# Turning round the up products of the dense feed-forwards

## The chip, the cores and the metric

One NeuronCore of a Trainium2 chip runs the whole program. The metric is the device time of an execution in microseconds. Three executions of the kernel before gave 2583.58, 2585.54 and 2586.75 us; the median is 2585.54.

## What is computed

Four transformer layers over 256 tokens of width 1024. Each has a mixer of four branches and then a feed-forward. Layers 1 to 3 have a dense one, layer 4 has eight experts, of which each token takes two. The change is about the three dense ones:

```
def swiglu(h, w_in, w_out):
    gate, up = jnp.split(h @ w_in, 2, axis=-1)
    return (jax.nn.silu(gate) * up) @ w_out
x = x + swiglu(rms_norm(x, g), w_in, w_out)      # hidden width 2816
```

`rms_norm` divides each token by the root mean square of its 1024 values and multiplies by a gain of each channel.

## The kernel before

**Precision.** Every large product is made of three in the fp32r form: with a = a_hi + a_lo and b = b_hi + b_lo, it adds a_hi b_hi, a_lo b_hi and a_hi b_lo. `hi` is a rounded copy, which ScalarE makes (`conv` in its program, recorded at line 1286, the helper's line), and `lo` the remainder, which VectorE makes (line 1685).

**The weight stream.** All weights are laid out as chunks of 128 x 2048 values (1 MB) in the order of use. SyncE loads them into a ring of six (`raw`); ScalarE makes `w_hi` in a ring of three; VectorE writes the remainder over the raw chunk. `conv(c + 2)` stands beside chunk c in both programs. TensorE waits for `lo_ready` of a chunk and counts `w_used` when done; that count releases ring places.

**Norm.** TensorE turns x into channel-major form, and ScalarE and VectorE write `xhi` and `xlo` (128 channels x 8 groups x 256 tokens) with the gain but without the division by the root mean square. ScalarE computes 1/rms of each token into `nstat` columns 4 and 5, token on the partition, after it has delivered `xhi`. So the factor is applied later, where a product leaves its PSUM bank.

**A dense stage.** The hidden width is cut into J = 11 blocks of 256. A block has two up chunks (each half of the 1024 input channels, for 256 gate and 256 up columns) and one down chunk (256 hidden rows by 1024 outputs). `feed_forward` in the programs of TensorE (line 1110), ScalarE (1568) and VectorE (2137) is driven by one order, `walk` (line 569): first up chunk of block j+1, turn of block j, second up chunk of block j+1, down chunk of block j. The middle blocks stand in a hardware loop of two blocks.

- Up (`gemm_half`, line 707): x is stationary, a 128 x 128 load for each group of channels and 128 tokens, and 512 weight columns move: 24 products in a chunk, recorded at lines 716 to 718. The result has tokens on partitions, one bank for each 128 tokens, gate in columns 0 to 255 and up in the others.
- Gating: ScalarE writes `silu` = Silu(gate x 1/rms) from PSUM, VectorE `gprod` = up x 1/rms x silu (line 2145), 128 tokens at a time; 1/rms is a value of each partition.
- Turn: TensorE transposes `gprod` in four 128 x 128 pieces (line 705) into the banks of the block, ScalarE rounds them to `ghi`, VectorE writes `glo` (line 2152).
- Down (`gemm_rows`, line 721): `ghi` and `glo` are stationary, 512 weight columns move, 24 products (lines 731 to 733), adding up in banks 4 to 7 over all blocks. In the last chunk each half of the columns is counted apart, and VectorE adds them to x.

Blocks take turns between banks 0, 1 and 2, 3; `claim`, `use`, `ev` and `fl` plan which use of a bank waits for which release. The routed experts have their own functions and lines (1185 to 1206, 2204, 2208). The narrow projection of the mixers (lines 806 to 808) multiplies 28 stationary weight columns by 256 moving tokens.

Of the kernel before, what the change touches and what calls it, by code (L numbers as in the profile page):

```python
# [15 lines left out]
P = 128  # L16
# [204 lines left out]
def program(nc, a, out, stop=99):  # L221

    ctx = ExitStack()
    with ctx:
# [33 lines left out]

        pick = sb("pick", [P, NT, P], at=u_at + 8192)
# [152 lines left out]
        silu_done, ghi_done = sem("silu_done"), sem("gated_hi")  # L412
        route_m, route_e = sem("route_max"), sem("route_exp")
# [27 lines left out]
        USE, FULL, CH, FFB, HALF = {}, {}, {}, {}, {}  # L441
# [35 lines left out]
        for k in phases:  # L477
# [32 lines left out]
            else:  # L510
                J = FFJ[k[0]]
                FFB[k] = ffb
                if k[0] == "moe":
# [12 lines left out]
                    JU, JF = [m - n for m, n in zip(uses, u0)], [m - n for m, n in zip(fulls, f0)]  # L526
                    claim((k, "turned"), X[2])
                    claim((k, "scatter"), X[2], X[3], 2, 3)
                    c += 2
                else:  # L530
                    for j in range(J):
                        for t in range(NT):
                            claim((k, "U", j), 2 * (j % 2) + t, streamed=True)
                            claim((k, "T", j), 2 * (j % 2) + t)
                    claim((k, "D"), *X, streamed=True)
                    HALF[k, "D"] = len(HALF) + 1
                    c += 3 * J
                    ffb += 2 * J
                    last_x = [(b, USE[(k, "D"), b] + 1) for b in X]
# [160 lines left out]
        def _(pe):  # L700
# [409 lines left out]
            def feed_forward(k, J):  # L1110
                c0 = CH[k]

                def up(j, it, c, half):
# [5 lines left out]
                    if half == 0:  # L1119
                        for b in banks:  # L1120
                            pe.wait_ge(free[b], use((k, "U", j), b) + 2 * it)
                    gemm_half(banks, c0 + c, 4 * half, half == 0, half == 1, it)

                def turn(j, it):
                    for t in range(NT):
                        b = gbank(j, t)

                        pe.wait_ge(free[b], use((k, "T", j), b) + 2 * it)
                        tr(bank[b][:, 0:P], gprod[:, t, 0:P])
                        tr(bank[b][:, P:2 * P], gprod[:, t, P:2 * P]).then_inc(full[b], 1)  # L1130

                def down(j, it, c):
# [6 lines left out]
                    gemm_rows(X, c0 + c, lambda kk, t: (ghi[:, kk, t, :], glo[:, kk, t, :]), j == 0, j == J - 1, it,  # L1139
                              by_half=j == J - 1)  # L1140

                walk(pe, J, lambda j, it, c: up(j, it, c, 0), turn, lambda j, it, c: up(j, it, c, 1), down)
# [133 lines left out]
        def _(act):  # L1276
# [291 lines left out]
            def feed_forward(k, J):  # L1568
                c0 = CH[k]

                def up_done(j, it, c):
                    conv(c0 + c + 2, it)
                    for t in range(NT):
                        act.wait_ge(w_used, c0 + c + 1 + 6 * it)
                        go(silu[:, t, :], bank[gbank(j, t)][:, 0:FB], ACT.Silu, scale=nstat[:, 4 + t:5 + t]).then_inc(silu_done, 1)

                def turn(j, it):
                    for t in range(NT):
                        b = gbank(j, t)
                        act.wait_ge(full[b], fl((k, "T", j), b) + it)  # L1580
                        go(ghi[:, :, t, :], bank[b][:, 0:FB].rearrange("p (a b) -> p a b", a=2), ACT.Copy).then_inc(ghi_done, 1)
# [88 lines left out]
        def _(dve):  # L1670
# [466 lines left out]
            def feed_forward(k, J):  # L2137
                c0, f0 = CH[k], FFB[k]

                def up_done(j, it, c):  # L2140
                    conv(c0 + c + 2, it)
                    for t in range(NT):
                        b = gbank(j, t)
                        dve.wait_ge(silu_done, f0 + 2 * j + t + 1 + 4 * it)
                        V.scalar_tensor_tensor(out=gprod[:, t, :], in0=bank[b][:, FB:2 * FB], scalar=nstat[:, 4 + t:5 + t],
                                               in1=silu[:, t, :], op0=ALU.mult, op1=ALU.mult).then_inc(free[b], 1)

                def turn(j, it):
                    for t in range(NT):
                        b = gbank(j, t)  # L2150
                        dve.wait_ge(ghi_done, f0 + 2 * j + t + 1 + 4 * it)
                        V.tensor_tensor(glo[:, :, t, :], bank[b][:, 0:FB].rearrange("p (a b) -> p a b", a=2),  # L2152
                                        ghi[:, :, t, :].bitcast(F32), ALU.subtract).then_inc(free[b], 1)
# [422 lines left out]
```

## Time and profile before

| | |
|---|---|
| median of three executions | 2585.54 us |
| profiled execution | 2585.76 us, span 2583.9 us |
| TensorE, its weight loads | 2509.5 us (97%), 2068.5 us (80%) |
| VectorE | 1818.7 us (70%) |
| ScalarE | 1521.9 us (59%) |
| GpSimd | 183.6 us (7%) |
| read from and written to HBM | 626.57 MB, 7.48 MB |

The profile is of one execution. PE is TensorE and PEld its weight loads, which overlap its products. A product's recorded length of 0.39 us is longer than the distance to the next start, as products are pipelined; distances between starts are what counts. Spans of the other engines are true lengths. "Idle before" is the time that an engine stood before an instruction, with the one that released it.

### The profile page before, as it was taken

How to read it: one execution, taken by the hardware profiler on the slowest of the kernel's cores; microseconds unless marked ns; L12 is line 12 of the kernel's file. 1: busy time of each engine (PE TensorE's matmuls, PEld its weight loads, DVE VectorE, ACT ScalarE, POOL GpSimd, SP SyncE). 2: the span in 40 equal slices, each digit the busy share in tenths (PEclk: the TensorE clock that was granted, in tenths of full speed). 3: DMA queues.
4: the chain of work that ended last, by engine and by line, in shares of the span. 5: the costliest groups of instructions: out<-in, count | busy, mean ns of one | idle time of the engine just before them, and what ended most of it. 6: DMA issues, size and time to landing. Idle time of an engine off the chain costs nothing.

```text
span 2583.9 us, 32235 instructions
## 1 busy us (share of the span) xinstructions
PE 2509.5 (97%) x11900; PEld 2068.5 (80%) x11900; DVE 1818.7 (70%) x1795; ACT 1521.9 (59%) x1581; POOL 183.6 (7%) x141
## 2 busy tenths in 40 slices
PE   6999999999999999999999998999999999999997
PEld 5888788788878878878888876888888888888876
DVE  5577754557775555665555467888888888888887
ACT  5455544454544354545445555777777777777766
POOL 0100200010020000020000012000000000000060
PEclk8999999999999999999999999999999999999999
DMA  6444455444445564545554455999999999999995
GB/s 220 147 147 163 166 192 183 161 160 151 163 163 187 187 205 151 180 164 179 193 181 161 163 179 206 364 370 383 380 377 374 376 385 376 383 368 386 373 361 224
DMA packets 90564, 635.24 MB, mean 246 GB/s; under 512 B 10477, under 2 KB 10853, under 8 KB 15472
## 3 DMA queue, kind: packets, MB, share of 16 engines
q1 hardware_dynamic: 85104, 617.41, 65.0%
q0 software_dynamic: 4896, 16.09, 1.8%
q8 instruction: 56, 0.92, 0.1%
q10 hardware_dynamic: 480, 0.59, 0.1%
q14 instruction: 28, 0.23, 0.0%
HBM read 626.57 MB, written 7.48 MB: 245 GB/s over the span
## 4 chain that ended last, share of the span: by engine, by line
PE 88%; DVE 4%; ACT 3%; issue 3%; DMA 1%; DVEq 0%; SPq 0%; ACTq 0%
PE bank L716 13%; PE bank L718 12%; PE bank L717 12%; PE bank L1206 7%; PE bank L1204 7%; PE bank L1205 7%; PE bank L1185 4%; PE bank L1187 4%; PE bank L1186 4%; PE bank L731 3%; PE bank L733 3%; PE bank L732 3%; PE bank L705 3%; DVE w_lo L1685 2%; ACT w_hi L1286 1%
## 5 line engine op out<-in xcount | busy, mean ns | idle before, releaser
L1685 DVE TENSOR_TENSOR w_lo<-raw,w_hi 128x2048 fp32r<-128x2048 f32 x586 | 1359.2, 2322 | 492.5 <-ACT w_hi L1286 480.0
L1286 ACT ACTIVATE w_hi<-raw 128x2048 fp32r<-128x2048 f32 x586 | 1121.6, 1915 | 269.2 <-PE bank L733 102.1
L716 PE MATMUL bank<-w_hi,xhi 128*128 128x512 f32 x1456 | 580.4, 399 | 13.2 <-DVE w_lo L1685 7.5
L718 PE MATMUL bank<-w_lo,xhi 128*128 128x512 f32 x1456 | 569.7, 391 | 0.0
L717 PE MATMUL bank<-w_hi,xlo 128*128 128x512 f32 x1456 | 569.4, 391 | 0.0
L1204 PE MATMUL bank<-w_hi,xhi 128*128 128x512 f32 x896 | 359.0, 401 | 2.4 <-DVE w_lo L1685 2.4
L1206 PE MATMUL bank<-w_lo,xhi 128*128 128x512 f32 x896 | 350.2, 391 | 0.0
L1205 PE MATMUL bank<-w_hi,xlo 128*128 128x512 f32 x896 | 349.5, 390 | 0.0
L716 PEld LDWEIGHTS bank<-w_hi,xhi 128*128 128x128 f32 x1456 | 274.9, 189 | 71.8 <-issue 12.5
L718 PEld LDWEIGHTS bank<-w_lo,xhi 128*128 128x128 f32 x1456 | 274.6, 189 | 58.9
L717 PEld LDWEIGHTS bank<-w_hi,xlo 128*128 128x128 f32 x1456 | 275.2, 189 | 54.0
L1206 PEld LDWEIGHTS bank<-w_lo,xhi 128*128 128x128 f32 x896 | 168.2, 188 | 35.7
L1204 PEld LDWEIGHTS bank<-w_hi,xhi 128*128 128x128 f32 x896 | 168.3, 188 | 35.3 <-DVE w_lo L1685 3.9
L1286 ACT ACTIVATE ghi<-bank 128x256 fp32r<-128x256 f32 x178 | 64.8, 383 | 219.2 <-PE bank L705 219.2
L1205 PEld LDWEIGHTS bank<-w_hi,xlo 128*128 128x128 f32 x896 | 168.7, 188 | 31.6
L1185 PE MATMUL bank<-w_hi,ghi 128*128 128x512 f32 x448 | 176.9, 395 | 10.7 <-DVE glo L2208 10.7
L1186 PE MATMUL bank<-w_hi,glo 128*128 128x512 f32 x448 | 175.1, 391 | 0.0
L1187 PE MATMUL bank<-w_lo,ghi 128*128 128x512 f32 x448 | 175.1, 391 | 0.0
L2447 POOL TENSOR_TENSOR u<-u,gates 128x512 f32<-128x512 f32 x32 | 61.1, 1938 | 705.6 <-DVE gates L2091 705.6
L1185 PEld LDWEIGHTS bank<-w_hi,ghi 128*128 128x128 f32 x448 | 84.5, 189 | 32.5 <-DVE w_lo L1685 12.3
L731 PE MATMUL bank<-w_hi,ghi 128*128 128x512 f32 x264 | 103.0, 390 | 3.3 <-DVE glo L2152 3.3
L733 PE MATMUL bank<-w_lo,ghi 128*128 128x512 f32 x264 | 102.8, 389 | 0.0
(364 smaller groups left out, 2462.8 us busy)
## 6 DMA issues: line engine op xcount, KB each, us to landing
raw<-in_wexpert SPq DMA_DIRECT2D x337, 1024.0 KB, 5.1
raw<-in_wdense SPq DMA_DIRECT2D x249, 1024.0 KB, 4.8
expert_rows<-y POOLq DMA_DIRECT2D x7, 512.0 KB, 4.5
expert_rows<-back POOLq DMA_DIRECT2D x3, 512.0 KB, 3.8
x<-in_x SPq DMA_DIRECT2D x2, 512.0 KB, 4.9
biasT<-bias_rows POOLq DMA_DIRECT2D x1, 1024.0 KB, 6.7
normal_rows<-hrow POOLq DMA_DIRECT2D x1, 1024.0 KB, 6.3
out<-hrow SPq DMA_DIRECT2D x2, 512.0 KB, 2.7
```

What stands on the lines that cost most here:

```text
L716: mm(bank[banks[t]][:, :], xhi[:, k0 + k, tok], wh, start=start and k == 0, stop=False)
L717: mm(bank[banks[t]][:, :], xlo[:, k0 + k, tok], wh, start=False, stop=False)
L718: last = mm(bank[banks[t]][:, :], xhi[:, k0 + k, tok], wl, start=False, stop=stop and k == 3)
L731: mm(b, xh, hi[:, h, o:o + 512], start=first and k == 0, stop=False)
L1185: mm(dst, ghi[:, m, 0, :], hi[:, h, w], start=first, stop=False)
L1186: mm(dst, glo[:, m, 0, :], hi[:, h, w], start=False, stop=False)
L1187: last = mm(dst, ghi[:, m, 0, :], lo[:, s, w], start=False, stop=final)
L1204: mm(bank[b][:, :], xhi[:, kt, 0:P], hi[:, h, w], start=kt == 0, stop=False)
L1205: mm(bank[b][:, :], xlo[:, kt, 0:P], hi[:, h, w], start=False, stop=False)
L1206: last = mm(bank[b][:, :], xhi[:, kt, 0:P], lo[:, s, w], start=False, stop=kt == KT - 1)
L1286: return nc.scalar.activation(dst, src, f, **kw)
L1685: V.tensor_tensor(lo[:, c % RAW, :], raw[:, c % RAW, :], hi[:, c % HI, :].bitcast(F32), ALU.subtract).then_inc(lo_ready, 1)
```

## The change

The up products swap operands. The 128 x 128 weight tile is stationary and 256 tokens of x move, so that a chunk has 48 products of 256 columns in place of 24 of 512. The result has hidden channels on partitions: the gate in one bank (two groups of 128 channels by 256 tokens), up in the other. The gated product is thus in the form that the down product needs, and the four transposes are gone. 1/rms of a token lies along the free axis now. A row of it on all partitions (`rrow`) is made once a stage: VectorE scales an identity by it (`diag`), TensorE multiplies that by ones after the first up chunk, VectorE copies the bank. Then VectorE multiplies gate and up by the row, ScalarE takes Silu of the scaled gate, VectorE multiplies, ScalarE rounds (`fhi`) and VectorE writes the remainder (`flo`), each over 128 x 512 values at once. The fourth layer's experts are as before. Cut to its core:

```diff
+        fhi = sb("fhi", [P, 2, S], F32R, at=u_at)
+        flo = sb("flo", [P, 2, S], F32R, at=u_at + 2048)
         ...
+                    claim((k, "rstd"), X[0])
                     for j in range(J):
                         for t in range(NT):
                             claim((k, "U", j), 2 * (j % 2) + t, streamed=True)
-                            claim((k, "T", j), 2 * (j % 2) + t)
@@ TensorE, up
-                    gemm_half(banks, c0 + c, 4 * half, half == 0, half == 1, it)
-                def turn(j, it):
-                    for t in range(NT):
-                        b = gbank(j, t)
-                        pe.wait_ge(free[b], use((k, "T", j), b) + 2 * it)
-                        tr(bank[b][:, 0:P], gprod[:, t, 0:P])
-                        tr(bank[b][:, P:2 * P], gprod[:, t, P:2 * P]).then_inc(full[b], 1)
+                    pe.wait_ge(lo_ready, i + 1 + 6 * it)
+                    for kk in range(4):
+                        row = 4 * half + kk
+                        for m in range(4):
+                            w = slice(kk * 512 + m * P, kk * 512 + m * P + P)
+                            o = bank[banks[m // 2]][:, m % 2 * S:m % 2 * S + S]
+                            mm(o, hi[:, h, w], xhi[:, row, :], start=row == 0 and m % 2 == 0, ...)
+                            mm(o, hi[:, h, w], xlo[:, row, :], start=False, ...)
+                            last = mm(o, lo[:, s, w], xhi[:, row, :], start=False, ...)
+                    last.then_inc(w_used, 1)
+                    if j == 0 and half == 0:
+                        b = X[0]
+                        pe.wait_ge(free[b], use((k, "rstd"), b))
+                        pe.wait_ge(diag_ready, DIAG[k])
+                        for t in range(NT):
+                            last = mm(bank[b][:, t * P:t * P + P], C("ones"), diag[:, t, :], start=True, stop=True)
+                        last.then_inc(full[b], 1)
@@ TensorE, down
-                    for t in range(NT):
-                        b = gbank(j, t)
-                        pe.wait_ge(free[b], ev((k, "T", j), b) + 2 * it)
+                    pe.wait_ge(glo_done, FFB[k] + j + 1 + 2 * it)
@@ ScalarE
-                        go(silu[:, t, :], bank[gbank(j, t)][:, 0:FB], ACT.Silu, scale=nstat[:, 4 + t:5 + t]).then_inc(silu_done, 1)
+                    b = gbank(j, 0)
+                    act.wait_ge(free[b], ev((k, "U", j), b) + it)
+                    go(fsilu[:, :, :], gscaled[:, :, :], ACT.Silu).then_inc(silu_done, 1)
@@ ScalarE, turn
-                        go(ghi[:, :, t, :], bank[b][:, 0:FB].rearrange("p (a b) -> p a b", a=2), ACT.Copy).then_inc(ghi_done, 1)
+                    if j > 0:
+                        act.wait_ge(w_used, c0 + 3 * j + 2 + 6 * it)
+                    act.wait_ge(prod_done, FFB[k] + j + 1 + 2 * it)
+                    go(fhi[:, :, :], fprod[:, :, :], ACT.Copy).then_inc(ghi_done, 1)
@@ VectorE
+                dve.wait_ge(norm_rstd, NORM[k])
+                for t in range(NT):
+                    last = V.tensor_scalar(diag[:, t, :], ident_t[:, :], nstat[:, 4 + t:5 + t], None, ALU.mult)
+                last.then_inc(diag_ready, 1)
+                def per_token(dst, b):
+                    return V.tensor_tensor(dst, bank[b][:, :].rearrange("p (m t) -> p m t", m=2),
+                                           rrow[:, :].unsqueeze(1).to_broadcast([P, 2, S]), ALU.mult)
@@ VectorE, behind the second up chunk
+                    if j == 0:
+                        wait_full((k, "rstd"), X[0])
+                        V.tensor_copy(rrow[:, :], bank[X[0]][:, 0:S]).then_inc(free[X[0]], 1)
+                        dve.wait_ge(free[X[0]], ev((k, "rstd"), X[0]))
+                    dve.wait_ge(w_used, c0 + c + 1 + 6 * it)
+                    per_token(gscaled[:, :, :], gbank(j, 0)).then_inc(free[gbank(j, 0)], 1)
+                    per_token(uscaled[:, :, :], gbank(j, 1)).then_inc(free[gbank(j, 1)], 1)
+                    dve.wait_ge(free[gbank(j, 1)], ev((k, "U", j), gbank(j, 1)) + it)
+                    dve.wait_ge(silu_done, f0 + j + 1 + 2 * it)
+                    V.tensor_tensor(fprod[:, :, :], uscaled[:, :, :], fsilu[:, :, :], ALU.mult).then_inc(prod_done, 1)
@@ VectorE, turn
+                    dve.wait_ge(ghi_done, f0 + j + 1 + 2 * it)
+                    V.tensor_tensor(flo[:, :, :], fprod[:, :, :], fhi[:, :, :].bitcast(F32), ALU.subtract).then_inc(glo_done, 1)
```

## Rows read from the trace of the kernel before

**Rows 1.** The page: engines' busy time (part 1) and the chain by engine (part 4).

```profile
PE 2509.5 (97%) x11900; PEld 2068.5 (80%) x11900; DVE 1818.7 (70%) x1795; ACT 1521.9 (59%) x1581; POOL 183.6 (7%) x141
...
PE 88%; DVE 4%; ACT 3%; issue 3%; DMA 1%; DVEq 0%; SPq 0%; ACTq 0%
```

**Rows 2.** Windows of the first dense stage: busy us and instructions, clock, DMA share, GB/s.

```profile
304.00:490.00 186.00, 184.45 (x834) 152.64 (x835) 96.55 (x84) 84.59 (x90) 0.00 (x0) 1.00 0.53 183
```

**Rows 3.** TensorE's timeline in that stage (start us, us, engine, line, operation).

```profile
326.81 0.39 PE L731 MATMUL bank<-w_hi,ghi 128*128 128x512 f32 x1
...
332.25 0.39 PE L716 MATMUL bank<-w_hi,xhi 128*128 128x512 f32 x1
...
337.69 0.60 PE L705 MATMUL bank<-ident_t,gprod 128*128 128x128 f32 x4
338.05 0.48 PE L716 MATMUL bank<-w_hi,xhi 128*128 128x512 f32 x1
338.36 0.39 PE L717 MATMUL bank<-w_hi,xlo 128*128 128x512 f32 x1
...
354.49 0.60 PE L705 MATMUL bank<-ident_t,gprod 128*128 128x128 f32 x4
```

**Rows 4.** The timeline at the last turn of that stage.

```profile
483.16 0.40 PE L733 MATMUL bank<-w_lo,ghi 128*128 128x512 f32 x1
...
485.08 0.47 PE L731 MATMUL bank<-w_hi,ghi 128*128 128x512 f32 x1 [1.09 <-DVE glo L2152]
```

**Rows 5.** Groups by line and form: count, busy us, mean ns, idle before.

```profile
L2135 DVE TENSOR_TENSOR x<-bank,x 128x512 f32<-128x512 f32 x16 | 10.0, 684 | 0.0
...
L1286 ACT ACTIVATE kq<-E 128x512 fp32r<-128x512 f32 x2 | 1.2, 616 | 0.0
...
L2025 DVE TENSOR_SCALAR P2m<-P2m,small 128x256 f32<-128x256 f32 x8 | 2.8, 348 | 0.0
```

**Rows 6.** TensorE's timeline, narrow projection: first, 24th, and the product behind.

```profile
23.92 0.28 PE L806 MATMUL bank<-xhi,wsm_hi 128*28 128x256 f32 x1
...
26.59 0.28 PE L808 MATMUL bank<-xhi,wsm_lo 128*28 128x256 f32 x1
26.71 0.40 PE L716 MATMUL bank<-w_hi,xhi 128*128 128x512 f32 x1
```

**Rows 7.** TensorE's timeline, 256 and 128 columns in turn: first of 16, next after.

```profile
198.75 0.28 PE L925 MATMUL bank<-tri,zhi 128*128 128x256 f32 x1
...
200.51 0.45 PE L716 MATMUL bank<-w_hi,xhi 128*128 128x512 f32 x1
```

**Rows 8.** The weight loads' timeline in the same stretch.

```profile
198.75 0.19 PEld L926 LDWEIGHTS bank<-tri,zhi 128*128 128x128 f32 x1
198.87 0.19 PEld L925 LDWEIGHTS bank<-tri,zlo 128*128 128x128 f32 x1
198.97 0.19 PEld L926 LDWEIGHTS bank<-tri,zlo 128*128 128x128 f32 x1
```

**Rows 9.** The timeline of all engines at the start of the first dense stage.

```profile
309.84 0.44 ACT L1286 ACTIVATE nstat<-nstat 128x2 f32<-128x2 f32 x2
310.01 0.39 PE L716 MATMUL bank<-w_hi,xhi 128*128 128x512 f32 x1
...
312.26 2.29 DVE L1685 TENSOR_TENSOR w_lo<-raw,w_hi 128x2048 fp32r<-128x2048 f32 x1 [6.34 <-ACT w_hi L1286]
```

**Rows 10.** TensorE's timeline, plain f32 products with a full load.

```profile
69.12 1.89 PE L835 MATMUL bank<-z,cst 128*128 128x256 f32 x8
70.66 0.58 PE L716 MATMUL bank<-w_hi,xhi 128*128 128x512 f32 x1
```

**Rows 11.** Timelines of ScalarE and VectorE in the block of rows 3.

```profile
327.74 1.92 ACT L1286 ACTIVATE w_hi<-raw 128x2048 fp32r<-128x2048 f32 x1
332.45 1.92 ACT L1286 ACTIVATE w_hi<-raw 128x2048 fp32r<-128x2048 f32 x1 [2.80 <-PE bank L733]
...
329.68 2.29 DVE L1685 TENSOR_TENSOR w_lo<-raw,w_hi 128x2048 fp32r<-128x2048 f32 x1 [1.29 <-ACT w_hi L1286]
```

More of the change, by code:

```diff
@@ L512, in program @@
                 FFB[k] = ffb
+                DIAG[k] = len(DIAG) + 1
+                NORM[k] = len([p for p in phases[:phases.index(k)] if p[0] == "norm"])
                 if k[0] == "moe":
@@ L537, in program @@
                     c += 3 * J
-                    ffb += 2 * J
+                    ffb += J
                     last_x = [(b, USE[(k, "D"), b] + 1) for b in X]
@@ L1120, in up @@
                         for b in banks:
-                            pe.wait_ge(free[b], use((k, "U", j), b) + 2 * it)
-                    gemm_half(banks, c0 + c, 4 * half, half == 0, half == 1, it)
-                def turn(j, it):
-                    for t in range(NT):
-                        b = gbank(j, t)
-                        pe.wait_ge(free[b], use((k, "T", j), b) + 2 * it)
-                        tr(bank[b][:, 0:P], gprod[:, t, 0:P])
-                        tr(bank[b][:, P:2 * P], gprod[:, t, P:2 * P]).then_inc(full[b], 1)
+                            pe.wait_ge(free[b], use((k, "U", j), b) + it)
+                    i = c0 + c
+                    s, h = i % RAW, i % HI
+                    pe.wait_ge(lo_ready, i + 1 + 6 * it)
[4 more added lines that the diff above has]
+                            o = bank[banks[m // 2]][:, m % 2 * S:m % 2 * S + S]
+                            mm(o, hi[:, h, w], xhi[:, row, :], start=row == 0 and m % 2 == 0, stop=False, skip_group_check=True)
+                            mm(o, hi[:, h, w], xlo[:, row, :], start=False, stop=False, skip_group_check=True)
+                            last = mm(o, lo[:, s, w], xhi[:, row, :], start=False, stop=row == KT - 1, skip_group_check=True)
+                    last.then_inc(w_used, 1)
[6 more added lines that the diff above has]
+                        last.then_inc(full[b], 1)
                 def down(j, it, c):
@@ L1135, in down @@
                             pe.wait_ge(free[b], use((k, "D"), b))
[L1136 to L1139 removed]
+                    pe.wait_ge(glo_done, FFB[k] + j + 1 + 2 * it)
+                    gemm_rows(X, c0 + c, lambda kk, t: (fhi[:, kk, t * P:t * P + P], flo[:, kk, t * P:t * P + P]), j == 0, j == J - 1, it,
                               by_half=j == J - 1)
[L1142 removed]
+                walk(pe, J, lambda j, it, c: up(j, it, c, 0), lambda j, it: None, lambda j, it, c: up(j, it, c, 1), down)
             def gather(k):
@@ L2140, in up_done @@
                 def up_done(j, it, c):
                     conv(c0 + c + 2, it)
[L2142 to L2146, printed above, removed]
-                def turn(j, it):
[L2149 to L2153, printed above, removed]
+                    if j == 0:
+                        wait_full((k, "rstd"), X[0])
+                        V.tensor_copy(rrow[:, :], bank[X[0]][:, 0:S]).then_inc(free[X[0]], 1)
+                        dve.wait_ge(free[X[0]], ev((k, "rstd"), X[0]))
```

14 lines of the change are left out of this document (8 added, 6 removed).

## The prediction

> **What bounds the kernel now.** I read the page first, then stages by windows, then TensorE's timeline inside one stage. The page shows TensorE busy for 97% of the span and 88% of the chain of waits on it, vector and scalar engines far behind [rows 1]. The three dense feed-forward stages are each about 186 us long; in the first TensorE is busy 184.45 us of 186 at a granted clock of 1.00 (2.4 GHz), VectorE 96.6 and ScalarE 84.6, DMA at 0.53 [rows 2]. So only what TensorE issues, or what makes it wait, counts there; a longer vector instruction costs nothing while it stays inside its slack.
>
> One steady block of a stage shows it [rows 3]. The 24 products of the down chunk start at 326.81 and the next chunk's first at 332.25: 5.44 us, 0.2267 us for each 512-column product, with its weight load hidden. From the first turn to the next, 337.69 to 354.49, a block takes 16.80 us. It holds 72 such products, 72 x 0.2267 = 16.32. The rest, 0.48 us, is the turn: four transposes from 337.69, and the product behind them, whose successor starts 0.31 us later instead of 0.227.
>
> **Part by part.** A stage has 11 blocks, 22 up chunks and 11 down chunks.
>
> *Turns removed.* Ten of the eleven turns stand in a stream that never waits, so each gives back 0.48 us less rounding, 0.475: 3 x 10 x 0.475 = 14.2 us. The eleventh, before the last down chunk, is different. Now the last product of block 9 starts at 483.16 and the last down chunk at 485.08 [rows 4], and the transposes lie inside a wait for copy and remainder. After the change the same place holds no transposes, but the rounding copy may start only when that product has ended (its buffer is single): 483.56 + ScalarE's copy of 512 columns 0.62 + VectorE's subtraction 0.68 [rows 5] + three handovers of about 0.05 = 485.0. Gain nothing. Nor is anything behind it: VectorE and ScalarE queue there only the next stage's first conversions.
>
> *Up products turned round.* Each up chunk had 24 products of 512 columns with a 128-column load of x; it gets 48 of 256 columns with a 128-column load of weights. Columns streamed stay the same, loads double. If t is the spacing of the new ones, the stages pay 66 x (48t - 24 x 226.7 ns), which is 3168 x (t - 113.35 ns). This one number decides the case, and no row shows exactly that product, so I bound it:
> - The narrow projection has the same form (weights stationary, hi twice, lo once, x moving, 256 columns) but loads 28 columns: 24 of them from 23.92 to 26.71, 116.25 ns each [rows 6].
> - Products of 256 and 128 columns in turn, both with 128-column loads: 16 from 198.75 to 200.51, 110 ns each [rows 7]. In the loads' own timeline a load beside a 256-column product is followed by the next after 0.12 us, one beside a 128-column product after 0.10 [rows 8]. So a full load needs less than the 113 ns, but with the wide product on top the pair takes up to 0.12.
> - Lower end: half of 226.7, 113.35 ns, since per column nothing in the stages is cheaper: cost 0. A gain below that is left out, as the columns are the same. Upper end: 120 ns, cost 21.1 us.
> I take 115.5 ns, nearest to the first row and a little under it, because that run is short and lies between wider products, and feed-forward stages are the steadiest stretches of the trace: 3168 x 2.15 = 6.8 us. Both ends go into the range.
>
> The rows show 0.2267 us for 512 columns [rows 3] and 116.25 ns for 256 [rows 6]. The Trainium skill (TensorE: Matmul & The Clock Gate, "Back-to-back issue gap") gives a warm gap of N/2.4 + 2.5 ns for an isolated product, 215.8 and 109.2 ns, so doubling the count would cost 2.5 ns for each old product, 4 us in all (an estimate from the page). The same section warns that in a stream of load and product pairs both set the spacing, and puts 128-column products at about 81 ns where the gap alone is 56; that speaks against this change, and is taken up below.
>
> *Changing width.* Where TensorE goes from short products back to 512-column ones the first steps are longer [rows 3]. This happens once in a block: 0 to 1.5 us in all, I take 1.0.
>
> *Scaling moved behind the product.* Token scales now lie along the free axis, so a row of them is made once a stage: VectorE waits for the reciprocal root, makes two diagonal tiles, TensorE multiplies them by ones after its first up chunk, VectorE copies the bank. The root's instruction ends at 310.06 (two in 0.44 us from 309.84) [rows 9]; two 128-column scalings at some 0.22 each (256 columns take 0.35 [rows 5]) end at 310.5, so TensorE can go on at 310.6. Its first chunk ended at 310.01. It stalls 0.6, runs two f32 products of 128 columns at 0.11 (eight of 256 take 1.54 us to the next start [rows 10]) and restarts its stream, 0.1 to 0.2: about 1.0 us a stage, 3.0 in all; 0.7 if the diagonal were ready, 4.5 if each handover took twice as long. Queued behind VectorE's new wait is its conversion of the third chunk, which started at 312.26 as ScalarE had not delivered before [rows 9], so it is not moved.
>
> *Vector and scalar work.* After an up chunk VectorE does two scalings of 512 columns from PSUM (0.68 each), ScalarE Silu of 512 from SBUF (0.62) beside the second, VectorE the product (0.68) [rows 5]: ready some 2.1 us after the chunk instead of 1.4. Before it, in queue, is the conversion at 327.74 on ScalarE and 329.68 on VectorE [rows 11]; they move by some 0.6 us. That conversion is for the chunk that TensorE begins at 338.05 [rows 3] and was done at 331.97: 6 us of slack. Rounding and remainder no longer wait for the transposes at 337.69 [rows 3]; they follow the conversion that ScalarE starts at 332.45 [rows 11], so they come earlier than now. TensorE's work covers all of this; without that cover it would be 0.6 us a block, 20 us. Banks come free earlier. DMA order and volume stay as they are.
>
> **Sum.** -14.2 + 6.8 + 1.0 + 3.0 = -3.4 us. The profiled execution took 2585.76 us with a span of 2583.9; that is 0.2 above the median of the three runs, 2585.54. The forecast is 2585.76 - 3.4 = 2582.4 us. About 0.2%, 5.2 us, is what a measurement can tell from no change. By the sum, the spacing gives a gain beyond that under 114.9 ns, and a loss beyond it over 118.2 ns.
>
> **Rivals.**
> *The split is free.* Long runs of short products settle at 113.35 to 114.5 ns. For: the stages' wide products hold 226.7 block after block [rows 3]; the load alone needs less. Against: 116.25 over 24 products in the narrow projection, at a much smaller load [rows 6]. Time 2575.6 at 113.35, up to 2579.2.
> *The load becomes the bound (slower).* Every product now has a full load beside its whole length. The load rows show 0.12 us for just this [rows 8], and if it holds for all 3168 the split costs 16 to 21 us where the turns give back 14.2. It decides from 118.2 ns on. At 118.5 the time is 2591.9, at 120 it is 2596.6. For: it is the only row with both sizes. Against: those loads follow short ones, and their first wide product has none of it.
> *The load is hidden only in part.* At 125 ns the split costs 36.9 us and the time is 2612.5. The run of 16 products at 110 ns speaks against it [rows 7]. The page's rule above, carried over as 25 ns on top of 109 (an estimate), would be 134 ns and some 65 us; this case's rows, at 116.25 with small loads, don't agree with it.
> *The gated product is late.* If remainders came after the down chunk's turn, each block would wait. Per block 1 us late gives 33 us, 2615. Against: 6 us of slack at each step.
> *That it doesn't do what it says* would be equal weights in a row loaded once, with only 32 loads in a chunk. The narrow projection's hi weights stand twice in a row too and each product there has its own load; it would only help, and is the free split.
>
> **Chances.** Forecast (114.9 to 118.2 ns) 0.39, own range 2580 to 2591; free split 0.36; load as bound 0.20; partly hidden 0.03; late product 0.02. So faster 0.36, same 0.39, slower 0.25. The range takes the free split and its uncertain small terms at one end and the load bound at 120 ns at the other: 2573 to 2597.
>
> **What would show it.** Right: transposes of the gated product gone from the dense stages, a block of 16.5 to 16.6 us with up products 115 to 116 ns apart, TensorE waiting once a stage for about 0.6 us on the diagonal, the last down chunk still starting some 1.9 us after the last product before it. Free split: blocks of 16.35. Load as bound: 16.9 and more, loads touching each other on TensorE's load row. The forecast is wrong if TensorE waits inside the loop for VectorE or ScalarE, if chunks after the first wait for conversions, or if the change of width costs more than 0.05 us a block.

## The result, and the profile after it

The changed kernel takes 2598.71 us (median of five runs, 2595.79 to 2599.49) against 2585.54 for the kernel before (five runs, 2583.58 to 2591.5). The ratio is 1.0048, 95% interval 1.0036 to 1.0059: slower by half a per cent. The forecast was 2582.4.

The page of the changed kernel, parts 1 and 4, answers to [rows 1]. TensorE has 1464 products more and 9 us more of busy time, VectorE 34 us more, and the chain lies on TensorE as before:

```profile
PE 2518.7 (97%) x13364; PEld 2139.8 (82%) x13364; DVE 1852.3 (71%) x1804; ACT 1514.5 (58%) x1515; POOL 188.7 (7%) x141
...
PE 87%; ACT 4%; DVE 4%; issue 3%; DMA 1%; DVEq 0%; SPq 0%; ACTq 0%
```

Its groups by line and form (busy us, mean ns, idle before). The up products, 3168 in three lines of 1056 each, wait 3.0 us in the whole program; the transposes of gated products fell from 356 to 224, the experts' own:

```profile
L1142 PE MATMUL bank<-xhi,w_hi 128*128 128x256 f32 x1056 | 299.1, 283 | 3.0 <-DVE xlo L1715 3.0
...
L743 PE MATMUL bank<-w_hi,fhi 128*128 128x512 f32 x264 | 103.4, 392 | 4.3 <-DVE flo L2184 4.3
```

The block of [rows 3] in TensorE's timeline. Line 743 begins a down chunk, line 1142 an up chunk:

```profile
328.43 0.40 PE L743 MATMUL bank<-w_hi,fhi 128*128 128x512 f32 x1
...
333.90 0.28 PE L1142 MATMUL bank<-xhi,w_hi 128*128 128x256 f32 x1
334.01 0.28 PE L1143 MATMUL bank<-xlo,w_hi 128*128 128x256 f32 x1
334.13 0.28 PE L1144 MATMUL bank<-xhi,w_lo 128*128 128x256 f32 x1
334.25 0.28 PE L1142 MATMUL bank<-xhi,w_hi 128*128 128x256 f32 x1
...
345.41 0.40 PE L743 MATMUL bank<-w_hi,fhi 128*128 128x512 f32 x1
```

From down chunk to down chunk 16.98 us, 16.80 before. The two up chunks fill 333.90 to 345.41: 11.51 us for 96 products, 119.9 ns each, without a wait or a transpose among them. Before, the same columns took 48 x 226.7 ns = 10.88 us and the turn 0.48. The weight loads go at the same pace, one for each product. Their records of 0.19 us are longer than the distance of 0.12 between them, so the loads' row has no gap any more:

```profile
350.99 0.19 PEld L1144 LDWEIGHTS bank<-xhi,w_lo 128*128 128x128 f32 x1
351.11 0.19 PEld L1142 LDWEIGHTS bank<-xhi,w_hi 128*128 128x128 f32 x1
```

Windows in up chunks (span, busy us of the loads, clock, DMA share, GB/s), the changed kernel first, then the kernel before:

```profile
335.00:345.00 10.00, 10.00 (x85) 1.00 0.63 211
```

```profile
333.00:337.00 4.00, 3.31 (x18) 1.00 0.81 266
```

The start of the stage, where the row of scales is made (compare [rows 9]), and the last turn ([rows 4]):

```profile
310.01 0.48 DVE L2162 TENSOR_SCALAR diag<-ident_t,nstat 128x128 f32<-128x128 f32 x2 [4.17 <-ACT nstat L1306]
310.09 0.28 PE L1144 MATMUL bank<-xhi,w_lo 128*128 128x256 f32 x1
...
310.64 0.68 PE L1151 MATMUL bank<-diag,cst 128*128 128x128 f32 x4 [0.27 <-DVE diag L2162]
311.08 0.36 PE L1142 MATMUL bank<-xhi,w_hi 128*128 128x256 f32 x1
...
486.49 0.39 PE L745 MATMUL bank<-w_lo,fhi 128*128 128x512 f32 x1
...
486.91 0.63 ACT L1306 ACTIVATE fhi<-fprod 128x512 fp32r<-128x512 f32 x1 [2.30 <-PE bank L745]
...
487.57 0.69 DVE L2184 TENSOR_TENSOR flo<-fprod,fhi 128x512 fp32r<-128x512 f32 x1 [0.64 <-ACT fhi L1306]
...
488.32 0.50 PE L743 MATMUL bank<-w_hi,fhi 128*128 128x512 f32 x1 [1.44 <-DVE flo L2184]
```

The second chunk starts 0.87 us late (311.08 against 310.09 + 0.12). The last turn takes 1.83 us, 1.92 before.

**Where the 13 us are.** I measure a dense stage from its norm's first transpose to that of the next norm. Before it is 189.47, 189.48 and 189.50 us; after, 192.84, 192.82 and 192.83. That is 10.0 us in all. The mixers between them are equal within 0.1 us, what lies ahead of the first within 0.4. The other 3.1 us of the two profiled spans lie in the expert stage (1005.73 and 1008.85), whose code is the same. TensorE's clock is part of it: windows there (columns: span, busy us of PE, PEld, DVE, ACT, POOL, clock, DMA share, GB/s) show 3.4 us at half clock (1.2 GHz). TensorE had stood idle for 3.0 us, up to 1623.83, and then worked for 1.2 us at the full clock. First the changed kernel:

```profile
1620.00:1625.00 5.00, 2.00 (x9) 1.39 (x8) 4.83 (x9) 2.47 (x3) 2.53 (x2) 1.00 0.96 377
1625.00:1628.40 3.40, 3.40 (x9) 2.62 (x9) 3.30 (x3) 0.04 (x1) 0.00 (x0) 0.50 0.49 159
```

The kernel before, at the same place, has the wait (2.8 us) and not the slow clock:

```profile
1610.00:1615.00 5.00, 2.21 (x10) 1.54 (x9) 4.90 (x6) 2.29 (x3) 1.20 (x2) 1.00 0.96 379
1615.00:1618.40 3.40, 3.40 (x17) 2.80 (x16) 2.89 (x3) 1.92 (x1) 0.00 (x0) 1.00 0.48 175
```

Nine products in 3.4 us instead of seventeen: 1.7 us for one such stretch. The changed kernel's five times themselves lie at 2595.8 and 2595.9 or at 2598.7 to 2599.5, and the profile is of one of the longer ones. So 10 us, those of the dense stages, are the edit's price for certain; whether it has a part in the 3.1 us of the expert stage is taken up in numbers 6 and 7.

### The profile page after: what moved, and what is told of

Read it like the earlier page. It is cut to its first block, busy times and chain, and to the rows that moved or that the text cites. A ratio compares the mean times of both kernels' runs of the same rounds, so it can differ in the third digit from the quotient of the medians.

```text
span 2597.1 us, 35091 instructions
## 1 busy us (share of the span) xinstructions
PE 2518.7 (97%) x13364; PEld 2139.8 (82%) x13364; DVE 1852.3 (71%) x1804; ACT 1514.5 (58%) x1515; POOL 188.7 (7%) x141
## 4 chain that ended last, share of the span: by engine, by line
PE 87%; ACT 4%; DVE 4%; issue 3%; DMA 1%; DVEq 0%; SPq 0%; ACTq 0%
PE bank L728 8%; PE bank L730 8%; PE bank L729 8%; PE bank L1226 7%; PE bank L1224 7%; PE bank L1225 7%; PE bank L1144 5%; PE bank L1143 5%; PE bank L1142 5%; PE bank L1205 4%; PE bank L1207 4%; PE bank L1206 4%; PE bank L743 3%; PE bank L744 3%; PE bank L745 3%
## 5 line engine op out<-in xcount | busy, mean ns | idle before, releaser
L728 PE MATMUL bank<-w_hi,xhi 128*128 128x512 f32 x928 | 371.5, 400 | 10.7 <-DVE w_lo L1705 8.0
L730 PE MATMUL bank<-w_lo,xhi 128*128 128x512 f32 x928 | 363.7, 392 | 0.0
L729 PE MATMUL bank<-w_hi,xlo 128*128 128x512 f32 x928 | 363.5, 392 | 0.0
L1224 PE MATMUL bank<-w_hi,xhi 128*128 128x512 f32 x896 | 359.2, 401 | 3.8 <-DVE w_lo L1705 3.8
L1226 PE MATMUL bank<-w_lo,xhi 128*128 128x512 f32 x896 | 350.2, 391 | 0.0
L1225 PE MATMUL bank<-w_hi,xlo 128*128 128x512 f32 x896 | 349.4, 390 | 0.0
L1142 PE MATMUL bank<-xhi,w_hi 128*128 128x256 f32 x1056 | 299.1, 283 | 3.0 <-DVE xlo L1715 3.0
L1144 PE MATMUL bank<-xhi,w_lo 128*128 128x256 f32 x1056 | 298.8, 283 | 0.0
L1143 PE MATMUL bank<-xlo,w_hi 128*128 128x256 f32 x1056 | 298.8, 283 | 0.0
L1142 PEld LDWEIGHTS bank<-xhi,w_hi 128*128 128x128 f32 x1056 | 202.6, 192 | 4.7 <-DVE xlo L1715 3.6
L1143 PEld LDWEIGHTS bank<-xlo,w_hi 128*128 128x128 f32 x1056 | 202.6, 192 | 1.1
L1144 PEld LDWEIGHTS bank<-xhi,w_lo 128*128 128x128 f32 x1056 | 202.6, 192 | 0.0
L1205 PE MATMUL bank<-w_hi,ghi 128*128 128x512 f32 x448 | 177.4, 396 | 10.4 <-DVE glo L2239 10.4
```

The costliest lines, as they stand in the source:

```text
L728: mm(bank[banks[t]][:, :], xhi[:, k0 + k, tok], wh, start=start and k == 0, stop=False)
L729: mm(bank[banks[t]][:, :], xlo[:, k0 + k, tok], wh, start=False, stop=False)
L730: last = mm(bank[banks[t]][:, :], xhi[:, k0 + k, tok], wl, start=False, stop=stop and k == 3)
L1142: mm(o, hi[:, h, w], xhi[:, row, :], start=row == 0 and m % 2 == 0, stop=False, skip_group_check=True)
L1143: mm(o, hi[:, h, w], xlo[:, row, :], start=False, stop=False, skip_group_check=True)
L1144: last = mm(o, lo[:, s, w], xhi[:, row, :], start=False, stop=row == KT - 1, skip_group_check=True)
```

## Experiments

Theory A: a 256-column product behind a full weight load is spaced at 120 ns, whatever the surroundings, so cutting a 512-column product in two costs 13.3 ns. Theory B: the 120 ns come from what is special here (which operand is stationary, banks, reads beside it). Theory C: the loss is not in TensorE's stream but in the longer chain of vector and scalar work or in the row of scales.

**1. Products alone.** A kernel of nothing but fp32r products, 48 of each width and load in a row:

```diff
+            for cols in (128, 96, 64, 32):
+                for width in (384, 320, 256, 192, 128):
+                    for _ in range(12): one(128, 512)
+                    for _ in range(48): one(cols, width)
```

> A kernel of its own, with TensorE alone at work: 48 fp32r products in a row for each pair of widths (stationary columns 128, 96, 64, 32; moving columns 512, 384, 320, 256, 192, 128), each product with its own load; it leaves the model's computation out. Theory A, a fixed price for each product that is fed by a full load: spacing is columns / 2.4 ns + 13.3, so 226.7 at 512, 173.3 at 384, 146.7 at 320, 120.0 at 256, and the load's own pace of 108 at 192 and 128; with narrower stationary tiles the price should shrink if it belongs to the load (about 110 at 256 x 32), and stay if it belongs to the product. Rival B, the load is the bound and is slowed by the product beside it: 120 at 256 but also about 120 at 192, and 384 and 320 at the proportional 170 and 142. Rival C, 120 is special to the feed-forward stages (other engines reading the same tiles): 113.3 at 256 here.

TensorE's windows of 5 us each (busy us, products, clock). The count is two or three above 5 us divided by the spacing, as products that began before are in it. This trace has no record of the clock, so that its column reads 1.00 throughout; that these windows are at the full clock shows in the opening products of 512 columns, which are 427 ns apart at first and 227 from 15.2 us on. In order: load of 128 columns beside 384, 320, 256 and 192 moving ones, then loads of 96, 64 and 32 beside 256:

```profile
28.00:33.00 5.00, 5.00 (x31) 1.00 0.01 3
37.00:42.00 5.00, 5.00 (x36) 1.00 0.00 0
47.00:52.00 5.00, 5.00 (x44) 1.00 0.02 3
55.10:60.10 5.00, 5.00 (x48) 1.00 0.00 0
92.30:97.30 5.00, 5.00 (x46) 1.00 0.00 0
135.50:140.50 5.00, 5.00 (x46) 1.00 0.00 0
177.20:182.20 5.00, 5.00 (x45) 1.00 0.01 3
```

Mean distance of starts over the last 36 of each run of 48, ns (512 with the full load: the opening products behind their slow start):

| load \ moving | 512 | 384 | 320 | 256 | 192 | 128 |
|---|---|---|---|---|---|---|
| 128 columns | 226.7 | 173.3 | 146.7 | 120.0 | 111.7 | 111.7 |
| 96 | 230.0 | 175.0 | 146.7 | 116.0 | 90.0 | 85.0 |
| 64 | 230.0 | 173.3 | 146.7 | 113.3 | 88.5 | 60.0 |
| 32 | 231.7 | 173.3 | 143.3 | 117.8 | 88.3 | 60.0 |

Theory A holds for the full load with no other engine at work: the spacing is columns / 2.4 GHz plus 13.3 ns at 512, 384, 320 and 256 columns, and 111.7 ns at 192 and 128, the same for both widths and so the load's own pace (108 was expected). That is against rival B, which had 120 at 192, and rival C, which had 113.3 at 256. What did not come out is that the price belongs to the load. At 320 columns and more a narrower load takes off 3.4 ns at most, and at 512 it adds 3 to 5; at 256 it takes off 6.7 ns at 64 columns, but only 2.2 at 32, where about 110 was expected. So the size of the load decides at 256 columns, not in general. And 256 columns beside the full load take 120.0 ns although 111.7 (the load's pace) and 113.3 (256 columns beside a load of 64) are both shorter.

**2. Only the split.** The kernel before, x stationary as ever, each 512-column up product cut in two:

```diff
-                    gemm_half(banks, c0 + c, 4 * half, half == 0, half == 1, it)
+                            for n in range(2):
+                                w = slice(kk * 512 + n * S, kk * 512 + n * S + S)
+                                o = bank[banks[t]][:, n * S:n * S + S]
+                                mm(o, xhi[:, row, tok], hi[:, h, w], ...)
+                                ...
```

> The kernel before, with each dense up product of 512 columns cut into two of 256; x stays stationary, the turns stay, nothing else changes. Theory A (the doubled number of loads and products is the whole loss, whichever operand is stationary): 120.0 ns between products, 66 chunks x 0.32 = +21.1 us, about 2606.7. Rival (the loss comes from having the weights stationary, or from the new vector chain): products at 113.4 ns and a time within 2 us of the kernel before, 2585 to 2588.

2608.39 us, ratio 1.0085, interval 1.0071 to 1.0099. Each dense stage is 196.26 us, 6.8 longer: 20.3 us. Its timeline has a block of 17.41 us, and 96 up products from 332.63 to 344.57 with a turn between:

```profile
327.16 0.40 PE L731 MATMUL bank<-w_hi,ghi 128*128 128x512 f32 x1
...
332.63 0.28 PE L1132 MATMUL bank<-w_hi,xhi 128*128 128x256 f32 x1
332.74 0.28 PE L1133 MATMUL bank<-w_hi,xlo 128*128 128x256 f32 x1
332.86 0.28 PE L1134 MATMUL bank<-w_lo,xhi 128*128 128x256 f32 x1
...
344.57 0.40 PE L731 MATMUL bank<-w_hi,ghi 128*128 128x512 f32 x1
```

The split alone, with turns kept and no new vector work, loses more than the whole change. Theory B's first part (the side that is stationary) is out; its others (banks, reads beside it) fell with number 1, which has 120.0 ns with nothing beside it.

**3. Only the turns taken out.** The kernel before without the transposes; the down chunk takes the gated product with tokens on partitions, so its values aren't those of the reference.

```diff
-                        tr(bank[b][:, 0:P], gprod[:, t, 0:P])
-                        tr(bank[b][:, P:2 * P], gprod[:, t, P:2 * P]).then_inc(full[b], 1)
+                    pass
```

> The kernel before without the dense transposes: the gated product is rounded straight from SBUF in token-major form, so the down product gets the untransposed matrix (this is the part left out). Up products are the 512-column ones. By my sum the 30 turns are worth 14.2 us and the last one of a stage nothing: 2571.3. Rival (turns lie partly beside other work and are worth less, so that they and not only the split explain the loss): 2574 to 2580.

2572.59 us, ratio 0.9947, interval 0.9934 to 0.9961. A stage is 184.5 us, 4.95 shorter: 14.9 us in all, of which the last turns give 0.7 (1.69 us instead of 1.92 each). The gain that the change was credited with is there; a steady block takes 16.32 us, 0.473 less than with its turn.

**4. The row of scales one chunk later.** The changed kernel, where TensorE takes the diagonal after its second up chunk:

```diff
-                    if j == 0 and half == 0:
+                    if j == 0 and half == 1:
```

> The changed kernel with the row of token scales made after the second up chunk of a stage in place of after the first, so that TensorE no longer waits for the diagonal. Theory: the stall of 0.55 us behind the first chunk goes in three stages, -1.3 us against the changed kernel, 2597.4, if the vector chain of the first block, which then begins 0.2 us later, stays covered. Rival: the row comes too late for the first block and the stall turns up before the first down chunk; no gain, 2598.7.

2596.03 us, ratio to the kernel before 1.0042 (1.0029 to 1.0056). The stages are 192.33, 0.5 shorter: the wait for the diagonal goes, its own products stay. That is 1.5 us in all, 1.3 expected. So the row costs little: 0.87 us a stage as it stood, 2.6 of the 10 us, of which this run gives back the 1.5.

**5. Wide where two share a load.** `x_hi` and `x_lo` beside each other, so that w_hi multiplies both in one product of 512 columns and only w_lo x_hi has 256. ScalarE and VectorE add the halves.

```diff
-                            mm(o, hi[:, h, w], xhi[:, row, :], ...)
-                            mm(o, hi[:, h, w], xlo[:, row, :], ...)
+                            mm(o[:, :], hi[:, h, w], xboth[:, :, row, :], ...)
-                            last = mm(o, lo[:, s, w], xhi[:, row, :], ...)
+                            last = mm(o[:, 0:S], lo[:, s, w], xhi[:, row, :], ...)
```

> The changed kernel, with w_hi multiplied by x_hi and x_lo in one product of 512 moving columns (two halves of a bank) and w_lo by x_hi in one of 256: 16 products of each kind in an up chunk in place of 48 of 256. A block fills four banks, the first block of a stage those of the down product; ScalarE copies the second halves out, VectorE adds them to the first; the row of token scales is made inside the second up chunk. Theory (a price of 13.3 ns for each product with a full load): 16 x (226.7 + 120.0) = 5.55 us a chunk against 5.76 in the changed kernel and 5.44 before; with the turns gone (-14.2), +7.0 for the chunks and +1.5 for the rows of scales the time is some 5.7 us under the kernel before, 2580.5. Rival: banks come free too late (copies and additions take 2.5 us behind each second up chunk, covered by 5.4 us of the down chunk), TensorE waits in each block, and it is no faster than the kernel before.

2596.69 us, ratio 1.0046 (1.0032 to 1.006): a miss by 16 us. Two things failed that the trace shows. In TensorE's timeline a pair takes 0.353 us, not 226.7 + 120.0 = 346.7 ns:

```profile
339.75 0.40 PE L1147 MATMUL bank<-xboth,w_hi 128*128 128x512 f32 x1
339.99 0.28 PE L1148 MATMUL bank<-xboth,w_lo 128*128 128x256 f32 x1
340.11 0.40 PE L1147 MATMUL bank<-xboth,w_hi 128*128 128x512 f32 x1
```

And the last turn took 3.01 us, as VectorE's remainder was queued behind a weight conversion that came too late to be done before it:

```profile
484.73 2.29 DVE L1721 TENSOR_TENSOR w_lo<-raw,w_hi 128x2048 fp32r<-128x2048 f32 x1 [1.04 <-ACT w_hi L1320]
486.94 0.68 DVE L2205 TENSOR_TENSOR flo<-fprod,fhi 128x512 fp32r<-128x512 f32 x1
```

The pairs cost 66 x 16 x 6.1 ns = 6.4 us and the last turns 3 x 1.2 = 3.5. Down chunks of 5.50 us, 5.44 before, account for about 2 more. The rest of the miss is not traced.

**6 and 7. Both kernels again**, unchanged, to see what the expert stage does by chance.

> The changed kernel once more, on the same chip as the run with wide hi products. The three dense stages should take 192.8 us each again, as they hang on 120.0 ns alone. The expert stage, whose code no edit touches, took 1005.7 us in the profile before and 1008.9 in the one after. If that is chance (the place of idle stretches in the clock's steps), it should come out anywhere from 1005 to 1009; if the change causes it, at 1008.5 to 1009 again.

> The kernel before once more, for a second profile: dense stages 189.5 us each. If the length of the expert stage is chance it lies anywhere from 1005 to 1009; if the change lengthens it, at 1005.7 again.

The changed kernel: 2595.97 us, ratio 1.004 (1.0027 to 1.0054), dense stages 192.84 again, expert stage 1009.38 in its profile. The kernel before: one run, 2583.86, stages 189.47, expert stage 1006.08. Both came out where the expectations put them if the change lengthens the expert stage, so these two runs do not show chance.

Other traces speak for it. Number 2, which is the kernel before but for the split, has 1008.29 there, and number 9 1008.77; number 4, the changed kernel but for the place of one step, has 1006.31, and the remaining ones 1005.2 to 1007.0. The four long stages (the two of the changed kernel, numbers 2 and 9) each have a stretch of 3.4 us at half clock some 36.5 us behind their start, and the eight others have none there. The ten times of the changed kernel in both sets fall in two groups, six at 2595.4 to 2596.3 and four at 2598.7 to 2599.5, and both its profiles are of the upper one. So the same kernel takes either time; what decides it is not shown, nor whether the change makes the longer one more likely.

**8. Products alone, second set.** Other widths, two widths in turn, and in groups of 16:

```diff
+            for width in (288, 240, 224): ...      # load of 128
+            for cols in (112, 80): ...             # beside 256 columns
+            one(128, 512); one(128, 256)           # in turn, then 16 and 16
```

> The kernel of products alone once more, with full loads: 48 products each of 288, 240 and 224 moving columns; 256 columns with stationary tiles of 112 and 80; 512 and 256 in turn; 16 of 512 and then 16 of 256, four times; 512 x 128 and 256 x 64 in turn. Theory A: 133.3 at 288, 113.3 at 240, the floor of 112 at 224; at 256 between 120 and 113.4 as the stationary tile shrinks. For the product pair of 512 and 256 columns, 352 ns in the kernel with wide hi products: if the turn-about of widths costs it, the pair in turn takes 352 here too and 16 and 16 in groups take 226.7 and 120.0 each; if other engines cost it, the pair takes 346.7 here.

Full loads: 131.7 ns at 288 columns (11.7 above columns / 2.4; 133.3 expected), 111.7 at 240 and 224. Beside 256 columns: 117.8 with a load of 112, 113.3 with 80. In turn, 512 and 256 take 353.3 a pair (236.3 and 117.0); in groups they settle at 226.7 and 120.0. So the 6 ns of experiment 5 come from changing width at each product, and grouping takes most of them away: with the first steps of each group in it, a group of 16 and 16 takes 347 to 348 ns for two products. The last part, 512 columns with the full load and 256 with a load of 64 in turn, takes 346.7 a pair (229 and 118). Each alone would give 226.7 + 113.3 = 340.0, so changing width costs 6.7 there as well.

**9. Half a load.** The changed kernel with stationary tiles of 64 columns; half of the hidden channels is left out, the number and width of products stay.

```diff
-                            w = slice(kk * 512 + m * P, kk * 512 + m * P + P)
-                            o = bank[banks[m // 2]][:, m % 2 * S:m % 2 * S + S]
+                            w = slice(kk * 512 + m * P, kk * 512 + m * P + 64)
+                            o = bank[banks[m // 2]][0:64, m % 2 * S:m % 2 * S + S]
```

> The changed kernel with stationary weight tiles of 64 columns in place of 128 in the dense up products; it leaves out half of the hidden channels. The number of products and the 256 moving columns stay. By the spacing kernel the products should be 113.4 ns apart and not 120.0, so a dense stage takes 1056 x 6.6 ns = 7.0 us less, 185.9 us. Rival (the loss comes with 48 products in place of 24 whatever they load): 120.0 ns and 192.8 us.

One run, 2579.64 us; stages 186.26, that is 6.6 less than the changed kernel. In the timeline three steps take 0.35 us; a steady block takes 16.35 us with 113.4 ns for each of its 96 up products:

```profile
333.65 0.28 PE L1142 MATMUL bank<-xhi,w_hi 128*64 128x256 f32 x1
333.77 0.28 PE L1143 MATMUL bank<-xlo,w_hi 128*64 128x256 f32 x1
333.88 0.28 PE L1144 MATMUL bank<-xhi,w_lo 128*64 128x256 f32 x1
334.00 0.28 PE L1142 MATMUL bank<-xhi,w_hi 128*64 128x256 f32 x1
```

With nothing changed but the columns of the stationary tile, the stage gets back nearly all of the 7.0 us that the split cost (22 x 0.32). That is the free split of the prediction, down to its block of 16.35 us. So the cause is in the stationary tile and not in the number of products: the full tile beside 256 columns costs 6.6 ns over 113.4. A tile of 64 columns is a smaller load and also half as many rows of output, and no run separates the two.

**10. Wide and grouped.** Experiment 5 with 16 products of 512 columns, then 16 of 256 in each chunk; the late conversion goes behind the last rounding and remainder.

```diff
-                            for m in range(4):
-                                last = part(kk, m)
+                        for wide in (True, False):
+                            for kk in range(4):
+                                for m in range(4):
+                                    last = part(kk, m, wide)
@@ ScalarE and VectorE, turn
+                    if j == J - 1:
+                        conv(c0 + 3 * J, 0)
```

> The kernel with wide hi products, with two edits: in an up chunk the 16 products of 512 columns come first and then the 16 of 256, and the last remainder of a stage is written before the conversion that stood ahead of it. Theory: in groups the products keep 226.7 and 120.0 ns, 5.55 us a chunk and not 5.64, which gives 22 x 0.09 = 2.0 us a stage, and the last turn loses the 1.2 us that it had more than in the changed kernel: 189.1 us a stage against 192.4, and a time about 10 us under the kernel with wide hi products in turn, 2586 to 2587. With the clock's chance that is the kernel before, within 0.2%. Rival: the price is the product's and not the order's: 192.4 less 1.2, a time of 2593.

2585.18 us, ratio 0.9996 (0.9986 to 1.0005): 11 to 13 us faster than the changed kernel (2595.97 and 2598.71), no different from the one before. Stages 189.22, as expected; an up chunk takes 5.55 us where number 5 has 5.64; last turn 1.83.

**11 and 12. The conversion moved forward on ScalarE, and number 10 again.**

```diff
@@ ScalarE, turn (VectorE as in number 10)
-                    if j == J - 1:
-                        conv(c0 + 3 * J, 0)
@@ ScalarE, after the down chunk before the last
-... conv(c0 + c + 2, it) if j != J - 2 else None
+... conv(c0 + c + 2, it)
```

> The grouped version with one move: ScalarE rounds the weights of the stage's last chunk before it rounds the gated product of the last block, where it is idle for 2.2 us (478.84 to 481.00); VectorE's part stays behind its remainder of the gated product. In the grouped run both of VectorE's conversions ended only at 487.9, and the additions to x, whose first half was ready at about 485.5, began at 487.87, so that the next stage's first product started 4.8 us after the last down product instead of 3.9 in the kernel before. Theory (that order is what the grouped version still loses): VectorE's conversions end at 486.7, the first additions come before the last down product ends, the distance is 3.9 us, each dense stage is 0.9 us shorter with what follows it, 2.7 us in all: 2582.5 us, ratio to the kernel before 0.9985. Rival (ScalarE's early conversion delays the rounding of the gated product or something behind it by as much): 2585, no change from the grouped version. Up products stay at 227.8 and 119.9 ns by both.

> The grouped version again beside it on the same chip, as the yardstick: 2585.2 us, ratio to the kernel before 0.9996 within its interval. If it comes out as low as the version with the early conversion, the move brings nothing.

2581.21 us, ratio 0.9985, interval 0.9976 to 0.9994; number 10 again 2584.61, ratio 0.9998 (0.9989 to 1.0007), on the same chip. This version beats the kernel before by 0.15% and the changed one, compared through the kernel before (0.9985 against 1.0040 to 1.0048), by about 0.6%. In VectorE's timeline both conversions follow at once behind the remainder, and the first additions to x come before the last down product. The second fence is TensorE's, from the last down product to the next stage's first:

```profile
483.68 0.69 DVE L2208 TENSOR_TENSOR flo<-fprod,fhi 128x512 fp32r<-128x512 f32 x1 [2.04 <-ACT fhi L1323]
484.29 4.49 DVE L1724 TENSOR_TENSOR w_lo<-raw,w_hi 128x2048 fp32r<-128x2048 f32 x2
488.70 1.28 DVE L2221 TENSOR_TENSOR x<-bank,x 128x512 f32<-128x512 f32 x2
```

```profile
489.82 0.39 PE L750 MATMUL bank<-w_lo,fhi 128*128 128x512 f32 x1
490.08 0.63 PE L722 MATMUL bank<-ident_t,x 128*128 128x128 f32 x4
491.08 1.62 PE L722 MATMUL bank<-ident_t,x 128*128 128x128 f32 x12 [0.37 <-DVE x L2221]
493.60 0.47 PE L733 MATMUL bank<-w_hi,xboth 128*128 128x512 f32 x1 [0.90 <-issue]
```

3.78 us, as in the kernel before, where number 10 has 4.79. Between the stages' first products lie 188.24 us, against 189.22 in number 10 and 189.72 in the kernel before.

## Why the prediction was wrong

| term, us | predicted | measured |
|---|---|---|
| turns | -14.2 | -14.9 alone (number 3), the last turns' 0.7 in it |
| up products turned round | +6.8 | +21.1, worked out with 120.0 ns; the split alone 20.3 (number 2) |
| changing width | +1.0 | about +0.7: 33 blocks of 16.98, where 5.44 + 96 x 0.1200 is 16.96 |
| row of scales | +3.0 | +2.6, 0.87 a stage |
| last turns | 0 | -0.3, 1.83 for 1.92 |
| vector and scalar work | 0 | 0, no wait of TensorE inside a stage |
| sum | -3.4 | +10.0 in the dense stages (the terms give 9.9, with the last turns' gain counted once), and 3.1 in the expert stage in these two profiles, cause open |

*The failed step* is the spacing t of the new products. It was taken at 115.5 ns and is 120.0. The number of products and the formula 3168 x (t - 113.35 ns) were right: at 120 ns they give 21.1 us and 2596.6, the time of the rival "the load becomes the bound", and the faster runs lie at 2595.4 to 2596.3. The prediction said that this one number decides the case and then gave 0.20 to the true one. That rival's name is not exact: with the same load, 192 columns are 111.7 ns apart, so the load's own pace is not 120. The 3.1 us of the expert stage, which put the first median at 2598.71, are in no term of the prediction.

Why it was taken too low: the narrow projection's 116.25 ns [rows 6] has a load of 28 columns, and I read it as an upper bound made loose by a short run. The table of number 1 shows that small loads beside 256 columns are not smooth (117.8 at 32 columns, 113.3 at 64), so that row said nothing on the full load. The row that had both sizes of the new product was in the loads' timeline: a full load beside a 256-column product, and 0.12 us to the next [rows 8]. I had it as an end of the range and weighed it less as only half of that stretch's products are such. Nor could its two decimals decide it: a difference of 0.12 us between rounded starts is anything from 110 to 130 ns. Read further into that stretch, the trace before has loads 0.12 and 0.11 us apart by turns, and product starts 0.17 and 0.06 apart:

```profile
199.15 0.33 PE L925 MATMUL bank<-tri,zhi 128*128 128x256 f32 x1
199.32 0.22 PE L926 MATMUL bank<-tri,zhi 128*128 128x128 f32 x1
199.38 0.33 PE L925 MATMUL bank<-tri,zlo 128*128 128x256 f32 x1
```

So the 110 ns [rows 7] is a mean of two very different steps, lowered by the short ones at its start (the settled pair takes 0.23 us, 114 ns each), and no bound for either.

*The reason "a full load needs less than 113 ns, so it is hidden"* is wrong although its number is right: the loads' own pace is 111.7 ns, and 256 columns beside a load of 64 take 113.3, but 256 columns with the full load take 120.0 (numbers 1, 8 and 9). What inside TensorE adds the rest no run here shows.

The Trainium skill (TensorE: Matmul & The Clock Gate, "LDWEIGHTS (loading the stationary operand)") gives columns / 1.2 ns, 106.7 for a full load; the floor measured here is 111.7. The Trainium skill's section "Back-to-back issue gap" on the same page warned that in a stream load and product set the spacing together. That warning is what happened; its size was not: number 1 has 120.0 at 256 columns where the isolated formula gives 109.2, and 111.7 at 128 columns with the full load where the page has about 81.

*Turns, row of scales, last turn, cover.* Right within 0.7 us each. The block that was predicted at 16.5 to 16.6 is 16.98, and the spacing makes the difference (96 x 4.5 ns = 0.43). The chain of the gated product was covered as said: the rounding at 335.92 and the remainder at 338.25 are done 6.5 us ahead of the down chunk at 345.41:

```profile
335.92 0.61 ACT L1306 ACTIVATE fhi<-fprod 128x512 fp32r<-128x512 f32 x1
...
338.25 0.68 DVE L2184 TENSOR_TENSOR flo<-fprod,fhi 128x512 fp32r<-128x512 f32 x1
```

## What to carry to other kernels

When TensorE is the bound, count products and their weight loads as well as columns: here every fp32r product of 256 to 512 columns with a full load pays 12 to 13 ns beyond its columns. So a layout that saves transposes but halves the moving width must save more than 13 ns for each product that it cuts in two. Price a product by a row with the same load and the same width, never by a smaller load or by the mean of a mixed run. If the layout is wanted for another reason, let operands that share a stationary tile move in one product of full width, keep products of one width together, and then look at what is queued ahead of the work that ends the stage: here the three together made of a loss of 10 to 13 us a gain of 4.

## What the hardware showed unexpectedly

- Beside 256 moving columns the spacing does not fall steadily with the load: 120.0, 117.8, 116.0, 113.3, 113.3 and 117.8 ns at 128, 112, 96, 80, 64 and 32 columns (numbers 1 and 8).
- Beside 512 moving columns a narrower load is no cheaper: 226.7 ns with 128 columns, 230.0, 230.0 and 231.7 with 96, 64 and 32 (number 1).
- Beside a full load, 240 columns cost 111.7 ns and 256 cost 120.0: a step of 8.3 for 16 columns.
- Changing between 512 and 256 columns at each product costs 6 to 7 ns a pair, 353 for 347; in groups of 16 about 1 ns or less is lost (numbers 5, 8 and 10).
- A wait of TensorE of 2.7 to 3.0 us in the expert stage was followed by 3.4 us at 1.2 GHz in four profiles and by none in eight; 1.7 us hang on that, in code that no edit touched.
